# A second seven-product pair in the last three feed-forward stages, and another order of the work around it

## The reference, cut to what matters

```python
def swiglu(x, w_in, w_out):
    gate, up = jnp.split(x @ w_in, 2, axis=-1)
    return (jax.nn.silu(gate) * up) @ w_out
...
x = x + 0.5 * swiglu(rms_norm(x, ffn1_norm_g[i]), ffn1_w_in[i], ffn1_w_out[i])
```

## Time and profile before

| | us |
|---|---|
| median of 3 runs | 1527.27 (1527.04 to 1528.38) |
| the profiled execution, its own time | 1527.58 |
| its span in the trace | 1525.9 |
| TensorE busy | 1515.7 |
| VectorE / ScalarE / GpSimd busy | 1110.0 / 867.3 / 263.8 |

### The profile page before, as it was taken

The page is one execution under the profiler, slowest core; times in us unless marked ns, Lnnn a source line. Parts: engine busy times, 40 slices in busy tenths (PEclk is TensorE's granted clock), DMA queues, the critical chain, the costliest instruction groups (busy, mean ns, idle before and its releaser), DMA issues.

```text
span 1525.9 us, 19569 instructions
## 1 busy us (share of the span) xinstructions
PE 1515.7 (99%) x7714; PEld 1281.9 (84%) x7714; DVE 1110.0 (73%) x1211; ACT 867.3 (57%) x1087; POOL 263.8 (17%) x216
## 2 busy tenths in 40 slices
PE   9999999999999999999999999999999999999998
PEld 7888888888888888888888888899988888888886
DVE  6687766556787568776776788599998568667875
ACT  7545554646455554556776455476887344454554
POOL 0222200001132122220001232100571000012220
PEclk9999999999999999999999999999999999999999
DMA  7997656446976699765416975666554665579762
GB/s 253 308 262 222 188 173 200 138 166 217 276 219 195 182 289 259 217 188 179 151 56 213 305 226 185 207 190 203 180 182 145 215 193 188 174 219 302 211 185 101
DMA packets 274307, 311.40 MB, mean 204 GB/s; under 512 B 64272, under 2 KB 233512, under 8 KB 274216
## 3 DMA queue, kind: packets, MB, share of 16 engines
q1 hardware_dynamic: 273112, 308.84, 65.4%
q10 hardware_dynamic: 1104, 1.31, 0.3%
HBM read 295.92 MB, written 1.09 MB: 195 GB/s over the span
## 4 chain that ended last, share of the span: by engine, by line
PE 94%; issue 2%; DVE 2%; ACT 1%; POOL 1%; DMA 1%; ACTq 0%; DVEq 0%; POOLq 0%
PE ps L2371 24%; PE ps L2375 24%; PE ps L2372 24%; PE ps L2413 3%; PE ps L2587 2%; PE ps L2588 2%; PE ps L2586 2%; PE ps L2361 2%; PE ps L2363 2%; PE ps L2362 2%; PE ps L2414 1%; PE ps L2429 1%; PE ps L2542 1%; DMA scr<-in_mem_dram 1%; PE ps L2693 0%
## 5 line engine op out<-in xcount | busy, mean ns | idle before, releaser
L1411 DVE TENSOR_TENSOR w_lo<-w_raw,w_hi 128x2048 fp32r<-128x2048 f32 x250 | 592.0, 2372 | 175.4 <-ACT w_hi L793 175.1
L793 ACT ACTIVATE w_hi<-w_raw 128x2048 fp32r<-128x2048 f32 x250 | 477.1, 1912 | 229.0 <-PE ps L2375 210.0
L2371 PE MATMUL ps<-w_hi,xg 128*128 128x512 f32 (+1 forms) x960 | 375.0, 391 | 0.0
L2375 PE MATMUL ps<-w_hi,xg 128*128 128x512 f32 (+1 forms) x960 | 372.1, 388 | 0.0
L2372 PE MATMUL ps<-w_lo,xg 128*128 128x512 f32 (+1 forms) x960 | 372.0, 387 | 0.0
L2371 PE MATMUL ps<-w_hi,y_hi 128*128 128x512 f32 x666 | 261.6, 393 | 0.5 <-DVE w_lo L1418 0.2
L2375 PE MATMUL ps<-w_hi,y_lo 128*128 128x512 f32 x666 | 259.1, 389 | 0.0
L2372 PE MATMUL ps<-w_lo,y_hi 128*128 128x512 f32 x666 | 258.9, 389 | 0.0
L761 POOL COPY scr<-scr 128x512 uint16<-128x512 uint16 x100 | 112.8, 1144 | 778.9 <-DVE scr L1526 778.9
L2371 PEld LDWEIGHTS ps<-w_hi,xg 128*128 128x128 f32 x960 | 180.3, 188 | 37.2 <-issue 0.7
L2375 PEld LDWEIGHTS ps<-w_hi,xg 128*128 128x128 f32 x960 | 180.2, 188 | 37.0
(11 more groups left out here) (409 smaller groups left out, 1864.1 us busy)
## 6 DMA issues: line engine op xcount, KB each, us to landing
w_raw<-in_ffn_w_in_dram SPq DMA_DIRECT2D x168, 512.0 KB, 4.9
w_raw<-in_ffn_w_out_dram SPq DMA_DIRECT2D x88, 512.0 KB, 4.8
w_raw<-in_w_in_dram SPq DMA_DIRECT2D x82, 512.0 KB, 4.5
w_raw<-in_a_w_in_dram SPq DMA_DIRECT2D x28, 512.0 KB, 4.6
w_raw<-in_w_down_dram SPq DMA_DIRECT2D x22, 512.0 KB, 4.5
w_raw<-in_w_gate_dram SPq DMA_DIRECT2D x21, 512.0 KB, 4.0
w_raw<-in_w_up_dram SPq DMA_DIRECT2D x21, 512.0 KB, 5.0
y_raw<-in_ffn_w_in_dram SPq DMA_DIRECT2D x16, 512.0 KB, 5.4
```

The source lines that it names most:

```text
L793: act.activation(w_hi[:, u % RING, :], w_raw[:, u % RING, :], ACT.Copy).then_inc(w_rounded, 1)
L1411: dve.tensor_tensor(w_lo[:, s, :], w_raw[:, s, :], w_hi[:, s, :].bitcast(F32), ALU.subtract).then_inc(w_split, 1)
L2371: pe.matmul(dst, xh, hi, start=start, stop=False, skip_group_check=True)
L2375: return pe.matmul(dst, xl, hi, start=False, stop=stop, skip_group_check=True)
```

## The change

The place of the pairs becomes a list for each stage: one pair at block 8 in ffn0 and ffn1, two pairs, at 4 and at 8, in ffn2, ffn3 and ffn4. The places of units come from the order of the steps. The preparation of a first pair is put into the three steps before it; a second pair's T blocks are loaded, and its T sums made, between the pairs. The lines removed are those of the kernel printed above.

```diff
-PAIR = 7
+PAIRS_OF = ((8,), (8,), (4, 8), (4, 8), (4, 8))
+def ffn_places(pairs):
+    order, i = [("G", 0, 0), ("G", 0, 1)], 1
+    while i < NI:
+        if i in pairs:
+            order += [("G", i, 0), ("G", i, 1), ("G", i + 1, 1), ("D", i - 1), ("G", i + 2, 0), ("G", i + 2, 1), ("D", i), ("D", i + 1)]
+            i += 3
+        else:
+            order += [("G", i, 0), ("G", i, 1), ("D", i - 1)]
+            i += 1
+    return {step: k for k, step in enumerate(order + [("D", NI - 1)])}
 SP
+                def block(p, k, j):
+                    half, i = ((0, p), (0, p + 1), (1, p + 1), (1, p))[k]
+                    if p == pairs[0]:
+                        sp.wait_ge(w_used, u + 1)
+                    else:
+                        sp.wait_ge(pe_done, pe_.at(f"M{(5, 7, 6, 4)[k]} {f} {pairs[0]}"))
...
+                def step(i):
+                    p = pairs[0]
+                    gate_up(1, i)
+                    if i == p - 2:
+                        block(p, 2, 0)
+                    down(i - 1)
+                    if i == p - 3:
+                        block(p, 0, 0)
+                    if i == p - 2:
+                        block(p, 2, 1)
+                    if i < NI - 1:
+                        gate_up(0, i + 1)
+                    turn_back(i - 1)
+                    if i == p - 3:
+                        block(p, 0, 1)
+                        block(p, 1, 0)
+                        block(p, 1, 1)
+                    if i == p - 2:
+                        block(p, 3, 0)
+                        block(p, 3, 1)
+                def pair(p):
+                    q = pairs[1] if p + 4 in pairs else None
+                    gate_up(1, p)
+                    gate_up(1, p + 1)
+                    down(p - 1)
+                    turn_back(p - 1)
+                    gate_up(0, p + 2)
+                    gate_up(1, p + 2)
+                    down(p)
+                    down(p + 1)
+                    turn_back(p)
+                    if q:
+                        for k in (0, 1):
+                            block(q, k, 0)
+                            block(q, k, 1)
+                    if p + 3 < NI:
+                        gate_up(0, p + 3)
+                    else:
+                        down(NI - 1)
+                    turn_back(p + 1)
+                    if q:
+                        for k in (2, 3):
+                            block(q, k, 0)
+                            block(q, k, 1)
 ScalarE, step(i)
                     round_(v + 2)
                     hidden_high(i - 1, (i - 1) % 2)
+                    if i + 1 == pairs[0]:
+                        t_high(i + 1, T2, "T2")
+                    if i + 1 in pairs[1:]:
+                        t_high(i + 1, T1, "T1")
                     round_(v + 3)
+                    if i + 2 == pairs[0]:
                         s_high()
                     for tt in range(2):
                         silu(i, tt)
+                    if i + 1 in pairs[1:]:
+                        t_high(i + 1, T2, "T2")
                     round_(v + 4)
+                    if i + 2 == pairs[0]:
+                        t_high(i + 2, T1, "T1")
 VectorE, step(i)
                     split(v + 2)
+                    hidden_low(i - 1, (i - 1) % 2)
+                    if i + 2 == pairs[0]:
+                        t_sum(i + 2, T1, T3, T1, "T1")
+                    if i + 1 == pairs[0]:
+                        t_sum(i + 1, T4, T4, T2, "T4", "T2")
+                        s_lows((0, 1))
+                    if i + 1 in pairs[1:]:
+                        t_sum(i + 1, T4, T4, T2, "T4", "T2")
                     split(v + 3)
                     for tt in range(2):
                         product(i, tt)
+                    if i == NI - 1:
+                        hidden_low(i, i % 2, tiles(ps[:, 6, :]))
+                    if i + 3 == pairs[0]:
                         x_sums()
+                    if i + 2 == pairs[0]:
+                        t_sum(i + 2, T3, T2, T3, "T3", "T1")
+                    if i + 1 in pairs:
+                        t_low(i + 1, T1)
+                        t_low(i + 1, T2)
                     split(v + 4)
+                    if i + 3 == pairs[0]:
+                        s_sums()
+                    if i + 2 == pairs[0]:
+                        t_sum(i + 2, T2, T2, T1, "T2", "T3")
 VectorE, pair(p): as before, and
                     split(n + 2)
+                    if p == pairs[0]:
+                        s_lows((2, 3))
...
                     split(n + 8)
+                    if p + 4 in pairs:
+                        t_sum(p + 4, T1, T3, T1, "T1")
+                        t_sum(p + 4, T3, T2, T3, "T3", "T1")
+                    if p + 2 == NI - 1:
+                        hidden_low(p + 2, p % 2, tiles(ps[:, 6, :]))
                     split(n + 9)
+                    if p + 4 in pairs:
+                        t_sum(p + 4, T2, T2, T1, "T2", "T3")
 all engines
+                while i < NI:
+                    if i in pairs:
+                        pair(i)
+                        i += 3
+                    else:
+                        step(i)
+                        i += 1
```

More of the change, by code:

```diff
@@ L84, in add @@
         opens.extend(c == "g" for c in pattern)
-    ffn = "d" * (3 * NI - 1)
+    ffn = ["d" * len(places) for places in PLACES]
     add("mem", "dddd")
-    add("ffn0", ffn)
+    add("ffn0", ffn[0])
     add("mixa", "ggggg" + "d" * 10)
     add("mixa_out", "d" * (A_OUT // 256))
-    add("ffn1", ffn)
-    add("ffn2", ffn)
+    add("ffn1", ffn[1])
+    add("ffn2", ffn[2])
     add("mixb", "d" * 7)
     add("mixb_out", "d" * (A_OUT // 256))
-    add("ffn3", ffn)
+    add("ffn3", ffn[3])
     add("dt", "g")
@@ L106, in plan_units @@
     add("w_o", "dddd")
-    add("ffn4", ffn)
+    add("ffn4", ffn[4])
     return first, opens
@@ L346, in build, with alone_until, alone @@
         T1, T3, T2, T4 = range(4)
+        def alone_until(f, i):
+            def alone(f, j):
+                return j not in PAIRS_OF[f] and j - 1 not in PAIRS_OF[f]
+            return sum(alone(g, j) for g in range(f) for j in range(NI)) + sum(alone(f, j) for j in range(i + 1))
         x_sum = tiles(KB(40, 8))
@@ L545, in ffn @@
                     small_inputs()
[L546 to L575, removed]
+                i = 1
+                while i < NI:
[5 more added lines that the diff above has]
+                        i += 1
+                if NI - 3 not in pairs:
+                    down(NI - 1)
                 if f == 4:
@@ L1655, in ffn @@
                     pass
-                for i in range(3, PAIR):
-                    step(i)
-                pair()
-                for i in range(PAIR + 3, NI):
-                    step(i, last=i == NI - 1)
+                i = 3
+                while i < NI:
+                    if i in pairs:
+                        pair(i)
+                        i += 3
+                    else:
+                        step(i)
+                        i += 1
             def mem(n, gain, factor):
@@ L2638, in ffn @@
                         pe.wait_ge(act_done, act_.at("M kT 1"))
-                    down(i - 1, start=i == 1)
-                pair()
-                for i in range(PAIR + 3, NI):
-                    gates(i, taken(i - 1))
-                    down(i - 1, hidden=(lambda: hidden(NI - 1)) if i == NI - 1 else None)
+                    down(i - 1, start=i == 1, hidden=(lambda: hidden(NI - 1)) if i == NI - 1 else None)
+                i = 1
+                while i < NI:
+                    if i in pairs:
+                        pair(i)
+                        i += 3
+                    else:
+                        step(i)
+                        i += 1
                 down(NI - 1, norm=n + 1)
```

253 lines of the change are left out of this document (111 added, 142 removed).

## The result

The changed kernel takes 1543.75 us (median of 5 runs, 1542.5 to 1545.29); the kernel before, run beside it on the same chip, 1527.54 (5 runs, 1527.04 to 1529.17). The ratio is 1.0103, with a 95% interval of 1.0089 to 1.0118: **16 us slower**, where I had forecast no change and had let the range end at 1534.

What follows compares the result with a forecast made beforehand. TensorE, almost never idle, was taken as the bound. The terms -8.2 + 6.1 + 0.9 + 1.5 = +0.3 gave 1527.6 by the median, stated as 1527.5 us; the range was 1520.5 to 1534.

Steps and rivals of the forecast that it cites:

- The products: TensorE in ffn2 to ffn4: one pair more in each stage removes 36 products in all, -8.2 us.
- Place 1: Down unit of block 1 in ffn2 to ffn4: block 1's turn lands 4.3 us later behind loads, +6.1 us.
- Rival A: Block 1's turn doesn't pay for the block loads, so its slack holds: about 1521.5 us, chance 0.33.
- Place 3: Down unit of block 5, between the pairs: late products and a turn behind loads, 0.5 us a stage, +1.5 us.
- Rival B: Block 5's turn is held by 3.1 MB, its down unit waits 2.0 us in three stages: 1532 us, chance 0.25.
- The clock: TensorE's granted clock: the forecast sum had no term for a fall to the 1.2 GHz level, 0 us.
- Rival D: Waits of several microseconds bring TensorE's clock down, +33 us after two waits in each of three stages: about 1560, chance 0.02.
- Place 2: VectorE's list up to block M5 of the first pair: T1's low part 0.3 us late a stage, +0.9 us.
- Edits at nothing: Second pair at 8, ffn0 and ffn1's reordered preparation, GpSimd's and ScalarE's queues: no new wait, 0 us.
- Rival C: ffn0 and ffn1: compressed T work makes the single pair 2 us late each, +4: 1531.5 us, chance 0.03.

Runs made afterwards that it cites:

- experiment 8: Changed kernel with both pairs' loads moved, X and S sums moved forward, and the X sums cut in two halves: 1521.18 us, ratio 0.9954.
- experiment 2: Kernel before, pair still at 7, with only the eight half-block loads of ffn2 to ffn4 issued early, around the turns of steps 1 and 2: 1533.71 us.
- experiment 3: Changed kernel with three of the first pair's half-block loads moved ahead of block 0's turn and one behind it: 1535.99 us.
- experiment 7: Changed kernel, both pairs' loads moved, X and S sums forward, second pair's T4 block loaded behind block 6's turn, its sum after T1's low part: 1525.04 us.
- experiment 1: Changed kernel without the second pair, one pair at 8 in all five stages: 1527.63 us, ratio 0.9996.
- experiment 4: Changed kernel with the second pair's T1 and T2 loads between the turns of blocks 3 and 4, T3 and T4 behind block 5's turn: 1534.8 us.

## Why the prediction was wrong

- **The products, -8.2: right.** 36 fewer, at an undisturbed pace of 0.227 us; experiment 8 gets 7.2 of it to the end.
- **Place 1, D1, +6.1: right in cause, and in size for the sum.** 1.97 + 1.13 + 2.40 = 5.5 us. In ffn2 GpSimd's join came at 568.21 against 562.68, which is 4.5 us later once the 1.0 of the later start is off; the bytes had said 4.3. Reckoned from D1's due time it was 4.5, 2.4 and 5.2 us later in the three stages, 4.1 in the mean, so that the near sum is luck in part. I gave ffn3 the longest stall, since it had the smallest slack; but there the turn had taken 7.8 us already before the change and grew by only 0.3. The rest of the lateness is that the turn is issued later, 9.7 us ahead of D1's due time where it was 11.5 to 11.8. GpSimd's cut just ahead of it takes 3.2 us beside the x sums, where it took 1.2 before. That isn't the cause: in experiment 2 the cut takes 1.2, and the loads alone hold the turn as long. Experiment 2 makes this wait by itself, experiment 3 removes it, with the cut at 3.2. Rival A (the turn doesn't pay) is refuted.
- **Place 3, D5, +1.5: the step that failed.** I had two prices for it, 2.3 by bytes and 0.8 by a row, and went to 0.5, "on the side of the row". Measured: 2.42, 2.88 and 1.23, in all 6.5 us. The row (4.55 us for a turn behind 2.1 MB) was read as a price per MB, but in it the down loads had been issued well before the turn (from 655.25 to 659.3, the turn at 661.80). In the new order the last of 3.1 MB was issued 0.3 us ahead of the turn. In ffn2 the turn took 7.9 us in place of 3.2, 4.7 more. The lateness of the products, which I had put at 2, was 2.2: block 4's turn was issued 15.8 us ahead of D5's due time, where the same turn was 18.0 ahead of it before. A shorter join of that block (1.41 us against 2.56) gave most of 1.2 back, so that block 5's turn was 1.3 late: 8.5 ahead, where it was 9.8. With a shorter way from join to low part (0.4): 1.3 + 4.7 - 0.4 - 3.2 = 2.4. Rival B had the mechanism and the size (2.0 a stage); in place 1 I had even worked with the rate that holds, and then didn't use it for place 3. D6, 0.8 in ffn4, is the same thing one turn on and wasn't in the sum; experiment 7, with less in front of that turn, has no such wait.
- **The clock, 0: wrong.** Rival D had a chance of 0.02 and the wrong shape: "after two waits in each of three stages +33". The fall is real, but it comes with some waits only and lasts some eight passes, which cost 1.4 to 1.7 us, three times, together 4.7 us. It is a surcharge on a wait and not a state for the rest of the stage. I had also written that no row shows a fall from idleness; the trace of before does show one, at its end: TensorE's last product ends at 1518.90 and the clock falls at 1522.58. The Trainium skill's statement that a lack of activity brings the half clock back (TensorE: Matmul & The Clock Gate, Part 1) is borne out by these rows in its direction.
- **Place 2, VectorE up to M5, +0.9: right for M5, but a wait behind it was left out.** M5 waits 0.45 and 0.44 in two stages, 0.9 in all. But I had given what stands behind it "0.3 to 1.5 us of slack", and the S low parts were late by 1.0 in two stages. Together 2.9 us. The count took splits at 2.20 to 2.29; in this stretch they took up to 3.37, the longest beside a copy of GpSimd (583.29).
- **Edits at nothing.** Right: at the pair at 8 of the changed kernel TensorE has no idle time over 0.25 us; ffn0 and ffn1 take what they took before, and experiment 1 shows the same for the order of the single pair, within 0.02 us a stage. Rival C is out.
- **Not in the sum:** 2.9 us that no wait and no fall explains, in distances a little too long. In kernel 8 not more than 1 us is left of it; its cause was not tried.

In the sum, the terms by their measured sizes are -8.2 + 5.5 + 6.5 + 0.8 + 2.9 + 4.7 + 2.9 = +15.1, with 1.3 of start and mixers +16.4, the difference of the two spans. So of the 16 us between forecast and result, D5 is 5.0, the clock 4.7, the block S3 2.0, D6 0.8, the small distances 2.9 and the start and mixers 1.3; D1 came 0.6 under its term. The range was too narrow in the same way: B and D don't exclude each other, since the longest waits bring the falls.

What stays open: why the turns themselves take 8.1 to 9.4 us (block 1) and 6.7 to 8.3 us (block 5) with the same number of bytes issued ahead of them. Nor was a turn issued from another engine's queue, which would tell whether it is held by its place in SP's queue or by DMA engines that are full whatever the queue; the experiments here moved loads and turns against each other in one queue. Two pairs in ffn0 and ffn1 were not tried: other work of these stages uses the T buffers' memory there.

## What to carry to other kernels

A small transfer on which an engine waits, in a queue that also carries bulk loads, cost here its own latency plus a time for the bytes that were issued ahead of it and hadn't drained yet; a row from a time when more of the queue had drained was no price for that. So before more loads go into a stage, list for each such transfer what is issued just ahead of it, and put the loads behind it, or far enough ahead; here the same instructions in another order gave back 16.6 us. And where TensorE is the bound, price a wait of over 2.2 us with a surcharge of 1.5 for the clock and one near 2 with a chance of it, and count a two-input operation of VectorE beside a GpSimd copy as a cost to one of the two.

## What the runs showed of the hardware

- **The granted clock.** In the feed-forward stages of these profiles, up to TensorE's last product, there are six falls to the 1.2 GHz level, each seven or eight passes long. They begin between 0.2 us before and 1.4 us after the end of a wait. The idle times of 2.24, 2.26 and 2.72 us in the changed kernel and of 2.53 in experiment 3 each came with one; so did one of 1.90 in experiment 2 and one of 1.84 in experiment 4, but not the two of 2.10 us in experiment 4, nor 1.78 in experiment 2 and 1.81 in the changed kernel. So near 2 us it is the one or the other. Every trace, that of before too, has one more fall at its end, after TensorE's last product.
- **A turn behind loads.** A turn takes 3.2 us from issue to GpSimd's start with a drained queue, 7.9 and 8.9 us (559.28 to 568.21) behind loads, and SP's own issue of it grows from 1.24 to 4.09 and 5.07 us, so that what follows in SP's list is late as well. The longest in ffn2 is that of block 6, 9.7 us (642.09 to 651.83, issue 5.91); it costs nothing there, since D6 isn't due before 656.05. The Trainium skill (DMA: Bandwidth & Descriptors, the section on queues, rings and completion order) says that each DMA engine takes the descriptors of a ring in their order. The rows agree, but don't show whether it is this order or the full engines that holds the turn.
- **GpSimd beside VectorE.** The same copy took 1.33 and 1.34 us beside an idle VectorE, and 2.40 beside an addition with two inputs in on-chip memory. It can be the other way round: beside a short sum of 128x512 in the changed kernel (ffn1, 446.64) the copy took 1.33, and the sum 1.79 in place of 0.68. The Trainium skill (GPSIMD Engine Reference, Specifications) lists the shared interface with VectorE, with contention for operations with two such inputs. The rows agree: removing the overlap removed the extra 1.06 us.
